# Input RMSNorm of a decoder block taken token tile by token tile, with the root on ScalarE, the parameter rows loaded last and the first value block inside that stage

## What is computed

```python
def rms_norm(x, g):
    x32 = x.astype(jnp.float32)
    y = x32 * lax.rsqrt(jnp.mean(x32 * x32, axis=-1, keepdims=True) + EPS)
    return (y * g.astype(jnp.float32)).astype(x.dtype)

u = rms_norm(x, g_mix[l])
z = u @ w_in                       # columns: xr, gr, q, k, v, fl, m_lru, m_attn
log_f = jax.nn.log_sigmoid(fl.astype(jnp.float32) + b_forget.astype(jnp.float32))
c = jnp.cumsum(log_f, axis=1)      # bias of the attention scores
log_a = -LRU_C * r * jax.nn.softplus(-lam.astype(jnp.float32))
```

## Time and profile before

| | us |
|---|---|
| median of 3 runs | 1732.43 |
| lowest and highest of them | 1730.15, 1733.16 |
| the profiled execution | 1734.18 |
| its span, first to last instruction | 1732.6 |
| its mean granted TensorE clock | 0.980 of full |

### The profile page before, as it was taken

The page is one execution under the profiler, slowest core; times in us unless marked ns, Lnnn a source line. Parts: engine busy times, 40 slices in busy tenths (PEclk is TensorE's granted clock), DMA queues, the critical chain, the costliest instruction groups (busy, mean ns, idle before and its releaser), DMA issues. The chain is left out here.

```text
span 1732.6 us, 22936 instructions
## 1 busy us (share of the span) xinstructions
PE 1639.1 (95%) x8288; PEld 1311.0 (76%) x8288; DVE 1240.4 (72%) x1505; ACT 897.4 (52%) x1038; POOL 132.7 (8%) x180
## 2 busy tenths in 40 slices
PE   6999999999999999999999999699999999999990
PEld 6888888888888898878878988566677777776660
DVE  6877776666449882277855426799988888888876
ACT  6333343334236751166642112377778777777863
POOL 1000000000011100022200000100000000001013
PEclk9999999999999999999999999799999999999995
DMA  5354453334245443567762511799999999999977
GB/s 172 86 172 158 158 169 111 102 103 136 98 146 149 137 126 105 206 249 243 241 202 98 170 42 61 255 394 397 392 399 394 397 398 390 399 390 398 397 298 273
DMA packets 187097, 399.00 MB, mean 230 GB/s; under 512 B 16576, under 2 KB 96592, under 8 KB 186000
## 3 DMA queue, kind: packets, MB, share of 16 engines
q1 hardware_dynamic: 172464, 336.96, 53.7%
q0 software_dynamic: 8384, 29.63, 5.7%
q10 hardware_dynamic: 6176, 31.46, 4.8%
HBM read 326.35 MB, written 71.65 MB: 230 GB/s over the span
## 5 line engine op out<-in xcount | busy, mean ns | idle before, releaser
L2060 DVE TENSOR_TENSOR e_l<-e_raw,e_h 128x2048 fp32r<-128x2048 f32 x192 | 439.1, 2290 | 65.0 <-ACT e_h L2054 64.4
L2054 ACT ACTIVATE e_h<-e_raw 128x2048 fp32r<-128x2048 f32 x192 | 367.9, 1917 | 90.9 <-PE ps L2089 40.8
L2076 PE MATMUL ps<-e_h,e_xth 128*96 128x512 f32 x512 | 205.1, 401 | 5.0 <-DVE e_l L2060 3.0
L2076 PE MATMUL ps<-e_h,e_xtl 128*96 128x512 f32 x512 | 202.7, 396 | 0.0
L2076 PE MATMUL ps<-e_l,e_xth 128*96 128x512 f32 x512 | 201.8, 394 | 0.0
L823 DVE TENSOR_TENSOR wn_stl<-wn_stl,ps 128x512 f32<-128x512 f32 x140 | 95.8, 684 | 56.2 <-PE ps L771 49.0
L223 PE MATMUL ps<-uh,w_h 128*128 128x512 f32 x384 | 121.2, 390 | 3.2 <-DVE v L490 2.2
L223 PE MATMUL ps<-ul,w_h 128*128 128x512 f32 x384 | 120.9, 389 | 0.0
L223 PE MATMUL ps<-uh,w_l 128*128 128x512 f32 x384 | 120.8, 389 | 0.0
L2076 PEld LDWEIGHTS ps<-e_h,e_xth 128*96 128x96 f32 x512 | 83.0, 162 | 45.0 <-issue 7.3
L2076 PEld LDWEIGHTS ps<-e_h,e_xtl 128*96 128x96 f32 x512 | 83.1, 162 | 36.2
(11 more groups left out here) (695 smaller groups left out, 3648.5 us busy)
## 6 DMA issues: line engine op xcount, KB each, us to landing
e_raw<-w_exp_gate SPq DMA_DIRECT2D x64, 1024.0 KB, 21.1
e_raw<-w_exp_up SPq DMA_DIRECT2D x64, 1024.0 KB, 21.0
e_raw<-w_exp_down SPq DMA_DIRECT2D x64, 1024.0 KB, 21.5
wn_raw<-w_in SPq DMA_DIRECT2D x40, 512.0 KB, 4.9
at_qk<-qk_d ACTq DMA_DIRECT2D x6, 2048.0 KB, 8.9
y_d<-e_y ACTq DMA_DIRECT2D x32, 384.0 KB, 6.5
y_d<-zeros POOLq DMA_DIRECT2D x22, 384.0 KB, 4.6
w_raw<-w_in SPq DMA_DIRECT2D x8, 1024.0 KB, 5.7
```

What stands on the lines that cost most here:

```text
L2054: act.activation(self.e_h[m % SPLIT][:, :, :], self.e_raw[slot][:, :, :], ACT.Copy).then_inc(self.e_hi[m % SPLIT], 1)
L2060: dve.tensor_tensor(self.e_l[slot][:, :, :], self.e_raw[slot][:, :, :], self.e_h[m % SPLIT][:, :, :].bitcast(F32), ALU.subtract).then_inc( ...
L2076: mm = pe.matmul(ps, x[:, k, :], w[:, k, :], start=first and first_piece, stop=last and last_piece)
```

## The change

The input norm works on one token tile at a time. g is loaded as rows, the same for every partition (`na_g`), behind the first tile of x; ACT takes the square root right after the square (no POOL); DVE inverts it and multiplies the tile with the inverse and with g in one instruction; PE turns the tile (eight transposes into one buffer of two banks); ACT copies the whole tile to the high part, DVE subtracts for the low part. The first value block's tile t is multiplied before tile t+2 is turned, so that tiles 0 to 5 lie in this stage and 6 and 7 in the next. The seven loads of parameter rows stand behind all of x, and their transpose, the copies and the whole softplus stand at the end of the stage.

```diff
         def sync(sp):
+            rows_in(0)
+            sp.dma_start(g_b[:, :], ins["g_mix"][0].partition_broadcast(P)).then_inc(g_loaded, 16)
+            rows_in(1)
+            k_.load_block(sp, 0, 0, k_.w_block(k_.w_in, VC))
+            for t in range(2, NT):
+                rows_in(t)
...
+            k_.load_block(sp, 1, 0, k_.w_block(k_.w_in, VC + WB))
         def scalar(act):
+            def root(t):
+                act.wait_ge(x_loaded[t], 16)
+                act.activation(square[:, :], xt[:, t, :], ACT.Square,
+                               accum_out=total[:, t:t + 1]).then_inc(squared, 1)
+                act.wait_ge(squared, t + 1)
+                act.activation(rstd[:, t:t + 1], total[:, t:t + 1], ACT.Sqrt, scale=1.0 / D, bias=eps[:, :]).then_inc(rooted, 1)
+            def high_part(t):
+                act.wait_ge(turned, t + 1)
+                act.activation(tokens(k_.uh, t), by_chunk(chunks(t)), ACT.Copy).then_inc(high, 1)
+            act.wait_ge(consts, 2)
+            root(0)
+            root(1)
+            high_part(0)
             k_.split_hi(act, 0, 0)
+            for t in range(1, NT):
+                high_part(t)
+                if t == 1:
+                    root(2)
+                if t + 2 < NT:
+                    root(t + 2)
+                if t >= 2:
+                    k_.value_high(act, 0, t - 2, st)
+            act.wait_ge(prm_turned, 1)
             act.activation(e[:, :], k_.prm[:, :, PS], ACT.Exp, scale=-1.0).then_inc(sp_exp, 1)
             act.wait_ge(sp_one, 1)
             act.activation(ln[:, :], w1[:, :], ACT.Ln).then_inc(sp_ln, 1)
         def tensor(pe):
+            def turn_rows(t):
+                pe.wait_ge(scaled, t + 1)
+                if t >= 2:
+                    pe.wait_ge(low, t - 1)
+                for k in range(KD):
+                    mm = pe.transpose(chunks(t)[:, k * P:(k + 1) * P], xt[:, t, k * P:(k + 1) * P], k_.ident[:, :])
+                mm.then_inc(turned, 1)
             pe.wait_ge(consts, 4)
+            turn_rows(0)
+            turn_rows(1)
+            for t in range(NT - 2):
+                pe.wait_ge(low, t + 1)
+                k_.value_tile(pe, 0, t)
+                turn_rows(t + 2)
+            pe.wait_ge(low, NT - 1)
             pe.wait_ge(prm_loaded, 16 * len(vectors))
             pe.transpose(turn, rows[:, :], k_.ident[0:n_rows, 0:n_rows]).then_inc(prm_mm, 1)
         def vector(dve):
+            def scale(t):
+                dve.wait_ge(rooted, t + 1)
+                dve.reciprocal(rstd[:, t:t + 1], rstd[:, t:t + 1]).then_inc(inverted, 1)
+                dve.wait_ge(inverted, t + 1)
+                dve.scalar_tensor_tensor(out=xt[:, t, :], in0=xt[:, t, :], scalar=rstd[:, t:t + 1], in1=g_b[:, :],
+                                         op0=ALU.mult, op1=ALU.mult).then_inc(scaled, 1)
+            def low_part(t):
+                dve.wait_ge(high, t + 1)
+                dve.tensor_tensor(tokens(k_.ul, t), by_chunk(chunks(t)), tokens(k_.uh, t).bitcast(F32),
+                                  ALU.subtract).then_inc(low, 1)
+            scale(0)
+            scale(1)
+            low_part(0)
+            k_.split_lo(dve, 0, 0)
+            for t in range(1, NT):
+                low_part(t)
+                if t == 1:
+                    scale(2)
+                if t + 2 < NT:
+                    scale(t + 2)
+                if t >= 2:
+                    k_.value_low(dve, 0, t - 2, st)
             dve.wait_ge(prm_mm, 1)
...
```

More of the change, by code:

```diff
@@ L243, in norm_in @@
         total = work.put("na_total", [P, NT])
-        mean = work.put("na_mean", [P, NT])
         rstd = work.put("na_rstd", [P, NT])
-        power = work.put("na_power", [P, NT])
+        eps = work.put("na_eps", [P, 1])
         n_rows = (CONV_W + 6) * KD
@@ L249, in norm_in @@
         e, w1, dw, ln, eq = (work.put(f"na_{n}", [P, KD]) for n in ("e", "w1", "dw", "ln", "eq"))
+        g_b = work.put("na_g", [P, D])
         x_loaded = [self.sem(f"na_x{t}") for t in range(NT)]
-        prm_loaded, prm_mm, prm_turned = self.sem("na_prm"), self.sem("na_prm_mm"), self.sem("na_prm_turned")
+        g_loaded, prm_loaded, prm_mm, prm_turned = (self.sem("na_" + n) for n in ("g_in", "prm", "prm_mm", "prm_turned"))
         consts = self.sem("na_consts")
-        squared, averaged, powered, scaled = (self.sem(f"na_{n}") for n in ("squared", "averaged", "powered", "scaled"))
+        squared, rooted, inverted, scaled = (self.sem(f"na_{n}") for n in ("squared", "rooted", "inverted", "scaled"))
         turned, high, low = self.sem("na_turned"), self.sem("na_high"), self.sem("na_low")
@@ L260, in norm_in @@
         vectors = [ins["conv_w"]] + [ins[n] for n in ("conv_b", "b_rg_a", "b_rg_x", "lru_lambda", "g_mix", "g_ffn")]
-        turn = k_.ps[3][:, HALF:HALF + n_rows]
-        chunk = lambda k: k_.ps[1 + k % 4 // 2][:, k % 2 * HALF:(k % 2 + 1) * HALF]
+        chunks = lambda t: k_.ps[1 + t % 2][:, :]
+        by_chunk = lambda ps: ps.rearrange("p (k n) -> p k n", n=P)
+        tokens = lambda u, t: u[:, :, t * P:(t + 1) * P]
+        turn = chunks(NT)[:, 0:n_rows]
         turn_v = turn.rearrange("p (v k) -> p k v", k=KD)
@@ L265, in sync @@
         def sync(sp):
[L266 to L278, removed]
@@ L279, in scalar, with rows_in @@
-        def scalar(act):
[L280 to L292, removed]
-            k_.split_hi(act, 0, 0)
[L294 to L301, removed]
+            def rows_in(t):
+                sp.dma_start(xt[:, t, :], k_.x[t * P:(t + 1) * P, :]).then_inc(x_loaded[t], 16)
@@ new lines, in sync @@
+            rows_in(0)
[4 more added lines that the diff above has]
+                rows_in(t)
+            row = 0
+            for src in vectors:
+                if src is vectors[0]:
+                    n, flat = CONV_W * KD, src.rearrange("a j (k p) -> (a j k) p", p=P)
+                else:
+                    n, flat = KD, src.rearrange("a (k p) -> (a k) p", p=P)
+                sp.dma_start(rows[row:row + n, :], flat).then_inc(prm_loaded, 16)
+                row += n
@@ L304, in scalar @@
             act.activation(ln[:, :], w1[:, :], ACT.Ln).then_inc(sp_ln, 1)
-            k_.value_high(act, 0, 3, st)
         def gpsimd(pool):
-            pool.memset(power[:, :], -0.5).then_inc(consts, 1)
+            pool.memset(eps[:, :], EPS).then_inc(consts, 1)
             pool.memset(k_.ones[:, :], 1.0).then_inc(consts, 1)
@@ L314, in gpsimd @@
                                base=0, pattern=[[1, P]], channel_multiplier=-1).then_inc(consts, 1)
-            for t in range(NT):
-                pool.wait_ge(averaged, t + 1)
-                pool.tensor_tensor(rstd[:, t:t + 1], mean[:, t:t + 1], power[:, t:t + 1], ALU.pow).then_inc(powered, 1)
         def tensor(pe):
-            pe.wait_ge(consts, 4)
+            def turn_rows(t):
[5 more added lines that the diff above has]
+                mm.then_inc(turned, 1)
+            pe.wait_ge(consts, 4)
+            turn_rows(0)
[5 more added lines that the diff above has]
+            pe.wait_ge(low, NT - 1)
             pe.wait_ge(prm_loaded, 16 * len(vectors))
             pe.transpose(turn, rows[:, :], k_.ident[0:n_rows, 0:n_rows]).then_inc(prm_mm, 1)
[L323 to L339, removed]
         def vector(dve):
@@ L343, in scale @@
             def scale(t):
[L344 to L362, removed]
+                dve.wait_ge(rooted, t + 1)
[7 more added lines that the diff above has]
+                                  ALU.subtract).then_inc(low, 1)
+            dve.wait_ge(g_loaded, 16)
+            scale(0)
[10 more added lines that the diff above has]
+                    k_.value_low(dve, 0, t - 2, st)
             dve.wait_ge(prm_mm, 1)
@@ L366, in vector @@
             dve.tensor_copy(k_.gf[:, :], turn[:, (PN + 1) * KD:(PN + 2) * KD]).then_inc(prm_turned, 1)
[L368 to L375, removed]
             dve.wait_ge(sp_exp, 1)
@@ L558, in tensor @@
         def tensor(pe):
-            pe.wait_ge(k_.u_low, 2 * KD)
-            for t in range(4, NT):
+            pe.wait_ge(k_.u_low, NT)
+            for t in range(NT - 2, NT):
                 k_.value_tile(pe, 0, t)
@@ L623, in vector @@
             u = lambda part, kk, th: k_.quarter(part, kk, th).bitcast(F32)
-            dve.wait_ge(k_.u_low, 2 * KD)
+            dve.wait_ge(k_.u_low, NT)
             dve.wait_ge(k_.softplus_own, 9)
@@ L629, in vector @@
             k_.split_lo(dve, 1, p0)
[L630 removed]
+            k_.value_low(dve, 0, 6, st)
             combine(spare(T4), u(k_.uh, 1, 1), u(k_.ul, 1, 1), ALU.add)
[L632 removed]
             combine(full(T1), spare(T3), u(k_.uh, 0, 0), ALU.subtract)
[L634 removed]
             combine(full(T1), full(T1), u(k_.ul, 0, 0), ALU.subtract)
```

1 line of the change is left out of this document (removed).

## The result

The changed kernel is slower: median 1738.01 us against 1731.96 for the kernel before in the same runs, ratio 1.0041 (95% interval 1.0029 to 1.0053), that is +6 us where +2.65 was forecast. It lies outside the forecast case "no change", on the side of the slower rival, and inside the stated range of 1731.0 to 1739.0. The profiled execution took 1739.62 us.

The account below looks back on a forecast made before the run. PE was taken to bind, DVE close behind; a 5.5 us head start is lost to waits, clock, transposes and DVE's later softplus, putting the transpose of the sums 2.65 later: 1735.1 us, range 1731.0 to 1739.0.

Parts of the forecast that it names:

- forecast case "no change": Whole kernel: time changes by under 0.2%, covering 1733.1 to 1735.9 us; chance 0.55.
- the slower rival: PE's clock falls at the wait for `sized`, 1.5 us a time, adding 0.5; over 0.2% (3.46 us) slower; chance 0.38.
- Rounds of 3.74: PE in the input norm: each round of a value tile (2.9) and eight transposes (0.84) takes 3.74 us.
- The load before the first root: ACT, first token tile: one table load of 1.28 us between first square and first root.
- the wait of 2.4 for the eighth low part: PE before value tile 6: idles some 2.4 us until DVE ends u's last low part at 43.05.
- from there to the sums 17.5: DVE from the `sized` step to the sums before `halves`: 17.54 us, where it took 18.81.
- The loss at the first tile of 2.2: PE's first value tiles: the lower clock costs 2.2 us, between bounds of 1.5 and 3.0.
- The softplus on the path: DVE between eighth low part and quarters of u: softplus stands there, so quarters start at 46.35, 6.3 us later.
- The next waited for its tile and starts at 5.90 ... ready at 5.69: ACT's first square: starts at 4.54, takes 1.15 us with its sum, ready at 5.69.
- a fall inside a stretch that DVE binds is mostly hidden: PE behind the wait for `sized`: a clock fall of 1.5 us adds only 0.5, given a margin of 1.0.
- The head start kept: PE reaches the transpose of the sums by 81.5, over 0.2% faster, 1728.1 us if DVE kept pace; chance 0.05.
- Transposes as a brake: PE's shorter rounds: transposes hold the clock at the lower level, some 15 us, 1750; chance 0.02.

Follow-up runs that it names:

- the same three edits: Changed kernel with a throw-away root ahead of the first tile, softplus moved to the start of `halves`, and eighth tile turned before value tile 5: ratio 0.9991 to the kernel before.

## Why the prediction was wrong

**What stood.** The argument that DVE's list behind the eighth low part decides this part: in the second profile the sums wait for it (0.34 idle), in the first PE comes 1.05 behind it, by the fall. Rounds of 3.74: measured 3.75 (27.65 - 23.90). The load before the first root; the wait of 2.4 for the eighth low part: 2.30; from there to the quarters 3.3: 3.4; from quarters to the forget step 23.5: 23.66; the wait there 2.4: 2.60; from there to the sums 17.5: 17.1. The loss at the first tile of 2.2: 5.21 - 2.9 = 2.3, though this is the high end, since the nine profiles give 1.3 to 2.3. The softplus on the path: shown by moving it, 3.4 down to 0.65 between the eighth low part and the quarters. The price of a table load of 1.3 without a drain: the root follows its load at 8.60, right behind 7.30 + 1.28.

**The term that failed first.** "The next waited for its tile and starts at 5.90 ... ready at 5.69", that is, the first square ends where it did. I priced one load before the first root and left the load that was already there at its place ahead of the data. A wait put at the head of ACT's list moved it behind the landing: +1.3, with 0.3 more for a later landing and 0.3 for the first eight transposes with their hand-on to ACT (2.1 from 10.48 to 12.61, where 1.8 was taken), and the first value tile came at 17.90 instead of 16.0. Moving that wait back gave 1.4; shown.

**The term that failed second.** It is "a fall inside a stretch that DVE binds is mostly hidden", by which a fall at the wait for the forget step was given 0.5 and left out of the sum. PE's margin against DVE at the sums was not 1.0 but 0.45 (89.54 against 90.59 - 1.5), since DVE was half a us faster on that way than I had it, and 1.05 of the fall's 1.5 came through. Two idle stretches were forecast, each longer than the one behind which the clock had fallen in the trace, so at least one fall belonged in the sum. Together: 1.9 + 1.05 = 2.95 over the 2.65, which gives the 5.6 measured at the sums; what else differed on DVE's way nearly cancels. That the fall goes with these waits is shown by the seven profiles with one and the seven without; its size at the sums, 1.05, rests on the first profile of the changed kernel, where the fall came behind the second wait, and in the second, with the fall behind the first, it adds nothing there.

**The rivals.** The slower one was right in mechanism, and in its place in the first profile (the clock falls behind the wait for `sized`; in the second it fell behind the other wait), but it too had the fall at 0.5 and no second table load. With the measured sizes either is enough to pass its bound of 3.46: 2.65 + 1.05 = 3.7, and 2.65 + 1.9 = 4.55. The head start kept: it was 3.65 at the first tile, and at tile 6 PE was 1.4 behind the kernel before (45.23 against 43.86), as argued. Transposes as a brake: from the second tile on, rounds of transposes and matmuls ran at 2.96 a tile, so not in this kernel. The Trainium skill ("TensorE: Matmul & The Clock Gate", section "Part 4: PE-mode transpose") says that transposes do not count as PE being busy in the same way; the trace does not agree. The 38 transposes ahead of the first value tile brought it to 2.94 in two profiles and 3.4 in a third, from 4.84 with the same three edits and without them, and 40 in the two waits kept the clock at 1.00. PE's timeline of the kernel with the 38, from its start:

```profile
1.84 5.38 PE L355 MATMUL ps<-ident,stri 128*128 128x128 f32 x24 [1.84 <-POOL stri L342]
8.23 1.10 PE L351 MATMUL ps<-ident,mix 128*128 128x128 f32 x8 [1.01 <-DVE mix L376]
```

The first 24 transposes take 0.22 each; the next eight take 1.10 together, at clock 1.00, and PE had done nothing but transpose until then. Without the 24 the same eight take 1.94. In the second profile of the kernel before, too, PE had only transposed before its first value tile, and that tile ran at the upper level from its start.

**The chances.** With the forecast 0.8 under the bound, and both unknown clock terms and unpriced details all on the slow side, 0.55 for "no change" was more than the rows carried.

## To carry to other kernels

A head start on the busiest engine is worth what the second busiest one allows: follow its list to the next signal, with its margin there, before counting it. Parameter work that nobody needs soon belongs in a stretch where its engine idles, not between the last producer and the first consumer of a stage. And look where the table load stands that is free in front of the data: here one more wait ahead of the first activation put it behind the data, and a throw-away activation of the function needed first, ahead of the wait for the data, kept it in front.

## What the runs showed that was not expected

PE's idle stretches of 1.8 to 2.9 us were followed by 3.4 us at clock 0.50 in some executions of a kernel and not in others of the same kernel: behind the idle ahead of the first value tile in one of two profiles of the kernel before, near 646 in one of two of the kernel with the transposes at the start, at the first or at the second wait in the changed kernel. Transposes of a constant tile kept the clock up behind a stretch each time that they left no gap over 0.5 us in it (at the forget step in two kernels, at the first wait in one, near 643 in one, one profile each); ahead of the first value tile, with gaps of 0.9 to 1.2 and of 1.7 to 1.8 left, the clock was at 0.50 for 3.4 us in two of three profiles, over by the first value tile, and from 9.8 to 16.7 in the third.

What stays open is why neither profile of the kernel before has a stretch at 0.50 near 650 or near 1030, while of the twelve profiles of the changed kernel and its variants eight have one near 650 and eight near 1030, eleven at least one of them, the exception being the one with transposes near 643. PE idles 1.8 to 2.9 ahead of the first place in all but the one with transposes there, and 2.3 ahead of the second in all of them, the kernel before among them. A fall there costs PE up to 1.5, so these falls may be part of why a shift at the sums and a difference in time differ by up to 2 us; that is not shown. Whether a changed start makes them more likely, or the two profiles of the kernel before were chance, is not settled.
